# Second-block attention rewritten as sigmoids and a running product, with v2 and cuv ahead of conv

## What is computed

```python
y_a = a_b * short_conv(a_c * a_h, conv_w)
q = rms_norm(q per head, q_norm_g); k = rms_norm(k per head, k_norm_g)
z = q k^T * 64 ** -0.5
causal = s_pos < t_pos
log_beta = log_sigmoid(z)
log_rem = where(causal, log_sigmoid(-z), 0.0)
suffix = cumsum(log_rem, reverse=True) - log_rem
weights = where(causal, exp(log_beta + suffix), 0.0)
y_b = weights @ v
y_c = gelu(c_u) * (tril(sgu_w) @ rms_norm(gelu(c_v), g) + sgu_b)
h = h + concat(y_a, y_b, y_c) @ w_out
```

## Time and profile before

| what | value |
|---|---|
| median of three runs | 1559.61 us (1556.6 to 1559.64) |
| the profiled execution | 1554.32 us, span 1552.6 us |
| PE busy | 1220.0 us (79%) |
| DVE busy | 532.4 us (34%) |
| ACT busy | 393.1 us (25%) |
| POOL busy | 25.4 us (2%) |
| chain that ended last | DMA 44%, PE 39%, DVE 13%, ACT 2% |

### The profile page before, as it was taken

One profiled execution on the slowest core, in us unless ns is written; L12 is line 12 of the kernel. 1 busy time (PEld: TensorE's weight loads), 2 busy tenths in 40 slices (PEclk: granted clock), 3 DMA queues, 4 the chain that ended last, 5 costly groups with the idle time before them and its releaser, 6 DMA issues.

```text
span 1552.6 us, 20288 instructions
## 1 busy us (share of the span) xinstructions
PE 1220.0 (79%) x8432; PEld 786.5 (51%) x8432; DVE 532.4 (34%) x951; ACT 393.1 (25%) x622; POOL 25.4 (2%) x43
## 2 busy tenths in 40 slices
PE   8988798986676676676776676775766888999998
PEld 8866687743233233233232232232233776899886
DVE  6999677511001001001001001001001866666546
ACT  5646644300100100100100100100100465455434
POOL 1000021000000000000000000000000000000000
PEclk9999999988878778778778778778688998999999
DMA  8563223899999999999999999999999433555550
GB/s 293 190 217 98 87 102 149 352 413 429 430 429 431 431 429 431 432 429 430 432 431 430 430 431 431 431 428 431 432 431 423 155 109 135 187 174 183 190 190 28
DMA packets 58753, 493.39 MB, mean 318 GB/s; under 512 B 6930, under 2 KB 8268, under 8 KB 34124
## 3 DMA queue, kind: packets, MB, share of 16 engines
q1 hardware_dynamic: 57756, 491.61, 77.5%
q10 hardware_dynamic: 944, 1.05, 0.2%
HBM read 491.59 MB, written 1.05 MB: 317 GB/s over the span
## 4 chain that ended last, share of the span: by engine, by line
DMA 44%; PE 39%; DVE 13%; ACT 2%; issue 2%; DVEq 0%; SPq 0%; ACTq 0%
DMA ring<-in_expert_w_down 14%; DMA arena<-in_expert_w_down 11%; PE ps L1644 9%; DMA ring<-in_expert_w_up 7%; DMA ring<-in_expert_w_gate 7%; PE ps L1731 7%; PE ps L2010 7%; PE ps L1649 5%; PE ps L1994 3%; DVE w_split L986 3%; DMA arena<-in_expert_w_up 2%; DMA arena<-in_expert_w_gate 2%; PE ps L2028 2%; DVE stat L1111 1%; PE ps L1710 1%
## 5 line engine op out<-in xcount | busy, mean ns | idle before, releaser
L986 DVE TENSOR_TENSOR w_split<-ring,w_split 128x1024 fp32r<-128x1024 f32 (+3 forms) x178 | 200.8, 1141 | 92.3 <-ACT w_split L598 91.2
L598 ACT ACTIVATE w_split<-ring 128x1024 fp32r<-128x1024 f32 (+3 forms) x178 | 174.3, 988 | 199.0 <-PE ps L1649 145.8
L2010 PE MATMUL ps<-arena 128*32 128x512 f32 x1024 | 156.7, 760 | 66.5 <-DMA arena<-in_expert_w_up 64.7
L2010 PE MATMUL ps<-ring,arena 128*32 128x512 f32 x1024 | 153.5, 745 | 64.3 <-DMA ring<-in_expert_w_up 62.6
L1405 DVE TENSOR_TENSOR arena<-arena,ps 128x512 f32<-128x512 f32 x16 | 11.0, 687 | 441.7 <-PE ps L2010 441.7
L1412 DVE TENSOR_TENSOR xs<-ps,xs 128x512 f32<-128x512 f32 x64 | 39.7, 682 | 290.2 <-PE ps L2036 290.2
L1994 PE MATMUL ps<-arena,xn 128*128 128x32 f32 x512 | 104.1, 381 | 43.4 <-DVE arena L1389 43.4
L1994 PEld LDWEIGHTS ps<-arena,xn 128*128 128x128 f32 x512 | 102.0, 309 | 49.6 <-DVE arena L1389 26.5
L2010 PEld LDWEIGHTS ps<-arena 128*32 128x32 f32 x1024 | 33.6, 130 | 182.1 <-DMA arena<-in_expert_w_up 98.1
L2010 PEld LDWEIGHTS ps<-ring,arena 128*32 128x32 f32 x1024 | 33.3, 128 | 177.6 <-DMA ring<-in_expert_w_up 96.8
L1731 PE MATMUL ps<-hT_hi,w_split 128*128 128x256 f32 x608 | 110.3, 284 | 1.6 <-issue 0.8
(11 more groups left out here) (354 smaller groups left out, 1414.0 us busy)
## 6 DMA issues: line engine op xcount, KB each, us to landing
arena<-in_expert_w_gate SPq DMA_DIRECT2D x35, 2048.0 KB, 35.5
ring<-in_expert_w_up SPq DMA_DIRECT2D x35, 2048.0 KB, 36.0
arena<-in_expert_w_up SPq DMA_DIRECT2D x29, 2048.0 KB, 36.9
ring<-in_expert_w_gate SPq DMA_DIRECT2D x29, 2048.0 KB, 36.4
arena<-in_expert_w_down SPq DMA_DIRECT2D x25, 2048.0 KB, 29.4
ring<-in_expert_w_down SPq DMA_DIRECT2D x21, 2048.0 KB, 30.6
ring<-in_w_ff SPq DMA_DIRECT2D x32, 1024.0 KB, 5.1
ring<-in_w_in SPq DMA_DIRECT2D x24, 1024.0 KB, 5.0
```

Source lines behind the costliest of these rows:

```text
L598: act.activation(w_split[:, n % WBUFS, 0, 0:cols], slot_view(slot, cols)[:, n % 2, :], ACT.Copy).then_inc(split_hi, 1)
L986: dve.tensor_tensor(buf[:, 1, :], w, buf[:, 0, :].bitcast(F32), ALU.subtract).then_inc(split_lo, 1)
L2010: m = pe.matmul(ps[j * CAP:(j + 1) * CAP, bank, :], xe[:, kt, :], w[:, r, j * FCOL:(j + 1) * FCOL], start=kt == 0, stop=kt == KT - 1, skip ...
```

## The change

Attention is computed with the query on the partitions and the keys reversed on the free axis. ACT takes sigmoid(-z) (`left`) and sigmoid(z) (`taken`) from the scores directly. DVE multiplies `left` along the row with one `tensor_tensor_scan` (state = left * state + whole_stick, where `whole_stick` is 1 at the start of each block row and 0 elsewhere, and `left` is 0 there), and one product with `taken` gives the weights. The mask is added on PE: a matmul of `ident_r` and `never` adds -2^126 above the diagonal. The weights then have queries on the partitions, so PE turns them by six transposes a pair, ACT copies them to `wT`, and PE multiplies by v2.

cuv comes before conv and has its own banks (1 and 3, "C"); conv is interleaved with the pairs alone. qk2 is no longer copied before it is squared; the two norm gains are vectors over the partitions now, applied while ACT copies the turned q. Of out2 the rows that pairs 0 and 1 fill come first, conv next. The gating product in bank 1 waits for `conv_middle`, the first of DVE's reads of conv, instead of all. The suffix matmuls, the masks `tri` and `later`, and the four clock-keeping matmuls ahead of the last pair are gone.

```diff
-                        ("conv", "w_in_2", 0, 768, D, "A"), ("cuv", "w_in_2", 2304, 512, D, "A"),
+                        ("cuv", "w_in_2", 2304, 512, D, "C"), ("conv", "w_in_2", 0, 768, D, "A"),
+        ROW_ORDER = {"out2": (1, 0, 2, 3)}
+        MIXED_AT = {"pair": (0, 1, 4, 5), "conv": (2, 3)}
@@ ACT
-            evac("qk2", (qk2[:, 0, :], whole))
...
-            act.activation(sq, qk2.rearrange("p h d -> p (h d)"), ACT.Square).then_inc(sq_ready, 1)
+            for h in range(HALVES):
+                act.activation(sq[:, h * D:(h + 1) * D], pset(SETS["qk2"], h), ACT.Square,
+                               scale=rstd_x[:, h:h + 1]).then_inc(sq_ready, 1)
             high_parts("v2", 3)
-            high_parts("conv", 0, 3)
...
+            high_parts("cuv", 0, 6)
+            act.activation(lam_s[:, 0:1], rstd_0[:, 0:1], ACT.Gelu)
+            high_parts("cuv", 6)
+            high_parts("conv", 0, 2)
...
+                act.activation(qkT2[:, j, 0:T], ps[:, 4 + j, 0:T], ACT.Copy, scale=qk_w2)
+                act.activation(qkT2[:, j, T:2 * T], ps[:, 4 + j, T:2 * T][:, ::-1], ACT.Copy).then_inc(qkT2_evac, 1)
...
+            gelus(0)
+            act.wait_ge(qk_w2_ready, 1)
+            turned_qk(0)
+            turned_qk(1)
+            gelus(1)
+            act.activation(lam_s[:, 0:1], rstd_0[:, 0:1], ACT.Sigmoid)
+            turned_qk(2)
+            turned_qk(3)
+            high_parts("conv", 2, 4)
+            act.wait_ge(stick_cleared, 1)
+            sigmoids(0)
+            def sigmoids(p):
...
+                act.activation(rest[:, :, 1:P], z[:, :, 0:P - 1], ACT.Sigmoid, scale=-1.0)
+                act.activation(rest[:, :, P + 1:SC], z[:, :, P:SC - 1], ACT.Sigmoid, scale=-1.0).then_inc(left_ready, 1)
...
+                act.activation(taken[p % 2].rearrange("p (m c) -> p m c", m=2), z, ACT.Sigmoid).then_inc(taken_ready, 1)
@@ DVE
+            roots(ss_d, rstd_d, 4 * SHEADS, SHD, between=lambda: low_parts("v2", 5, 6))
+            low_parts("v2", 6, 7)
+            for h in range(HALVES):
+                n = slice(2 * SHEADS * h, 2 * SHEADS * (h + 1))
+                step(dve.tensor_scalar(rstd_d[:, n], rstd_d[:, n], rstd_x[:, h:h + 1], None, ALU.mult))
+            scaled_qk(0)
             low_parts("v2", 7)
+            dve.wait_ge(row_done, 1)
+            dve.tensor_copy(root_row, ps[:, 3, 0:T]).then_inc(row_read, 1)
+            low_parts("cuv", 0, 1)
+            scaled_qk(1)
+            low_parts("cuv", 1, 2)
+            evac_v2(0)
+            low_parts("cuv", 2, 3)
+            evac_v2(1)
+            low_parts("cuv", 3)
             low_parts("conv", 0, 3)
...
+            def conv_middle():
+
+                dve.wait_ge(tile_used, done("conv"))
+                dve.tensor_tensor(a_hT, a_c, r2, ALU.mult).then_inc(conv_read, 1)
...
+            def stick_weights(p):
...
+                dve.tensor_tensor_scan(stick, left[p % 2], whole_stick, 0.0, ALU.mult, ALU.add).then_inc(left_read, 1)
...
+                dve.tensor_tensor(blocks[0][:, :, ::-1], blocks[1], blocks[2], ALU.mult).then_inc(w_ready, 1)
...
+            low_parts("conv", 3, 4)
+            dve.wait_ge(stick_cleared, 1)
+            stick_weights(0)
+            low_parts("conv", 4, 6)
+            gating_sums()
+            stick_weights(1)
+            low_parts("conv", 6, 7)
+            split_pair(0)
+            gating_scale()
+            stick_weights(2)
+            low_parts("conv", 7)
+            split_pair(1)
+            low_parts("out2", 0, 1)
+            stick_weights(3)
+            low_parts("out2", 1, 2)
+            conv_middle()
+            split_pair(2)
+            conv_inputs()
+            low_parts("out2", 2, 3)
+            convolution(0)
+            convolution(1)
+            split_pair(3)
@@ PE
+            pe.wait_ge(diag_ready, HALVES)
+            pe.matmul(ps[:, 3, 0:T], ones[:, :], diag, start=True, stop=True).then_inc(row_done, 1)
             tiles("v2", hT)
...
+            pe.wait_ge(row_read, 1)
+            tiles("cuv", hT)
+            pe.wait_ge(qk2_ready, HALVES)
...
+                        pe.matmul(ps[:, 4 + m, at_col:at_col + width], qkT2[r, p, t0:t0 + P], qkT2[r, p, 2 * T - width:2 * T], start=True, stop=False)
+                        last = pe.matmul(ps[:, 4 + m, at_col:at_col + P], ident_r[:, :], never[:, :], start=False, stop=True)
...
+            tiles_T("conv", [0])
+            pe.wait_ge(qkT2_evac, 2)
+            pair_scores(0)
+            tiles_T("conv", [1, 2])
+            pair_scores(1)
+            pe.wait_ge(qkT2_evac, 4)
+            pair_turned(0)
+            tiles_T("conv", [3])
+            pe.wait_ge(gelu_done, 4)
+            pair_output(0)
+            pair_scores(2)
...
+            pair_turned(3)
             pe.wait_ge(pw_ready, 1)
             pe.wait_ge(cv_ready, 1)
-            pe.wait_ge(gelu_done, 4)
+            pe.wait_ge(conv_read, 1)
```

More of the change, by code:

```diff
@@ L423, in load_vec @@
                 src = t[name]
-                if name.startswith("diff"):
+                if name in HALF_ROWS:
+                    src = src if name.startswith("diff") else src[0:1]
                     for i in range(2):
@@ L528, in corner @@
             return pset(SETS[name], h)[:, j * 512:(j + 1) * 512]
+        raw_mask = hid[:, 0:P]
         @block.gpsimd
@@ L876, in _ @@
-            act.wait_ge(tile_used, done("cuv"))
-            for h in range(HALVES):
-                src = pset(SETS["cuv"], h)
-                act.activation(cv2[:, h, :], src[:, SGU:2 * SGU], ACT.Gelu, scale=rstd_x[:, h:h + 1]).then_inc(gelu_done, 1)
-                act.activation(u2[:, h, :], src[:, 0:SGU], ACT.Gelu, scale=rstd_x[:, h:h + 1]).then_inc(gelu_done, 1)
+            high_parts("cuv", 0, 6)
+            act.activation(lam_s[:, 0:1], rstd_0[:, 0:1], ACT.Gelu)
+            high_parts("cuv", 6)
@@ L886, in _ @@
+            sigmoids(1)
+            turned_weights(0)
+            high_parts("conv", 6, 7)
+            sigmoids(2)
+            high_parts("conv", 7)
+            turned_weights(1)
+            high_parts("out2", 0, 1)
+            sigmoids(3)
+            high_parts("out2", 1, 2)
+            turned_weights(2)
+            high_parts("out2", 2, 3)
+            turned_weights(3)
             high_parts("out2", 3, 7)
@@ L946, in step, with roots @@
                 dve.wait_ge(dve_step, count[0])
-            def roots(ss, out, n, dim, ready=None):
+            def roots(ss, out, n, dim, ready=None, between=None):
                 v, a, y = nw[0][:, 0:n], nw[1][:, 0:n], nw[2][:, 0:n]
@@ L960, in roots @@
                         step(last)
+                    if k == 0 and between is not None:
+                        between()
                 last.then_inc(ready, 1) if ready is not None else None
@@ L1610, in mixed @@
             def mixed(kt):
-                return (y_conv, kt + 1) if kt < 2 else (y_pair, kt - 1) if kt < 6 else (y_gate, 1)
+                for part, counted in (("pair", y_pair), ("conv", y_conv)):
+                    if kt in MIXED_AT[part]:
+                        return counted, MIXED_AT[part].index(kt) + 1
+                return y_gate, 1
             def transpose_bank(src, base, b, halves):
@@ L2134, in _ @@
             m.then_inc(sv_done, 1)
-            tiles("out2", yT, [4], ready=lambda kt: pe.wait_ge(*mixed(kt)))
+            y_part = lambda kt: pe.wait_ge(*mixed(kt))
+            pe.wait_ge(taken_ready, SHEADS // 2)
+            pair_output(3)
+            tiles("out2", yT, [0], ready=y_part)
+            tiles("out2", yT, range(1, 5), ready=y_part)
             pe.wait_ge(yc_ready, SG)
@@ L2140, in _ @@
             m.then_inc(ycT_done, 1)
-            tiles("out2", yT, range(5, KT), ready=lambda kt: pe.wait_ge(*mixed(kt)))
+            tiles("out2", yT, range(5, KT), ready=y_part)
             tiles("proj", pT)
```

288 lines of the change are left out of this document (128 added, 160 removed).

## The result

The changed kernel takes 1547.5 us (median of seven runs, 1541.84 to 1552.02) against 1556.6 us (1553.17 to 1559.64) for the kernel before in the same session: ratio 0.9938, 95% interval 0.9921 to 0.9955, so 9.1 us less where 21.2 were forecast. The time itself lies 0.5 us above the upper end of the range that the prediction gave, 1547. Of the distance to the forecast of 1538.4, 3.0 us go the other way: the forecast started from a median of three runs of the kernel before, 1559.61, and seven runs have 1556.6. The profiled execution took 1550.9 us with a span of 1548.7; the one before had 1552.6.

The account below looks back on a forecast made before the run. Back-and-forth between engines was taken as the limit. Terms A, B and C in a row ended at 1311.3 against 1336.6, 25.3 us less; with allowances 21.2 less, so 1538.4 us, range 1531 to 1547.

Parts of the forecast that it names:

- term B: DVE's own queue from the first scan until the gating product may start: 20.9 us, ending at 1278.5.
- at nothing: Small extra loads at the start, masks on GpSimd, its memsets and out2's new chunk order, all forecast to cost nothing.
- Term A: From qk2's end at 1225.0 until the first running product can start on DVE, forecast at 1257.6.
- its cover: PE's own queue alongside DVE's (conv tiles, scores, masks, turnings, outputs), forecast to reach 1278.0, level with DVE.
- rival 1: Each running product on DVE takes a second cycle an element, 3.2 us more on term B: 1541.6; chance 0.32.
- Term C: PE from the gating product to the end of the 16 "ff" transposes: 32.8 us.
- a slow stretch after stalls: Allowance for one stretch of slow PE clock after stalls of 1 to 2 us before the gating product: 3.4 us.
- Rival 2: PE stays at 1.2 GHz for two stretches more, 2 x 3.4 us: 1545.2; chance 0.12.
- Rival 3: No early release: gating product held by something else, PE waits for all conv_inputs (2.1 us): 1540.5; chance 0.05.

## Why the prediction was right and wrong

**Direction and mechanism: right.** The back-and-forth of the engines was the limit, and it is gone: PE idles 0.9 us after the end of qk2 where it had 15.2. The size was not right: the second block gave 16.4 of the 21.2, and the experts took 7.7 back. Two steps failed, the price of scores and masks in term B and the small vectors that were put at nothing.

**Term A: right.** The first scan was to start 32.6 us after qk2's end and started 32.1 after (1271.13 less 1239.0); cuv ended 23.8 after it, for 23.5. The table switch cost 1.28 us with the next call 0.02 behind, as the row of before had it. The drain that the Trainium skill (ScalarE: Activation LUTs, What ACT_TABLE_LOAD costs) adds does not show here.

**Term B: its cover failed.** I wrote "four scores with 16 mask matmuls of 0.06 to 0.17, so 3.4 + 1.6", and let DVE and PE be level at about 1278. The gating product started 62.2 us after qk2's end (1301.22 less 1239.0) where PE's queue gave 53.0: 9.2 late. The four pairs took 3.02 each and not 1.26, 7.0 in all. Clock is 1.7: 0.79 over 5 us and 0.67 over 2 is 1.2 GHz for 2.1 and 1.3 us. The two add to 8.7; the other 0.5 was not traced. The error was to take 0.86 for a pair's scores from rows in which four of them stand together, the two heads side by side, and a price per mask from rows in which matmuls of one kind follow one another, and to use both where two kinds alternate.

**The scan: rival 1's price was right, and it did not matter.** It takes 1.75 us, not the 0.96 I had taken. By this the trace agrees with the half throughput that the Trainium skill (DVE: opcode table, instruction layouts, handler registers and perf-mode slots, Datapath and trigger behaviour) states. But PE was the later of the two, so even a plain product moved nothing. Rival 1 reached 1541.6 by a path that was not the one that decides. DVE did have idle time between its scans, against what I wrote.

**Term C: right.** 32.8 forecast, 32.9 measured.

**The clock.** I allowed 3.4 us for a slow stretch after stalls. A loss of 1.7 came, while PE was without a gap. Rival 2's two stretches more did not come. Its reason was misread, too: PE did not stay at 1.2 GHz "after each stall over 1.5 us". The window from 1225 to 1245 holds a wait of 1.64 and has a clock of 1.00, and so has the one from 1287 to 1302, with a wait of 1.60 in it:

```profile
1294.30 0.73 PE L1649 MATMUL ps<-w_split,hT_hi 128*128 128x512 f32 x2 [1.60 <-DVE w_split L986]
```

**Rival 3, the early release: excluded.** In one profile it was worth 5 us and not the 2.1 of three products, since a loss of 3.3 by the clock came on top of the wait of 1.7; that the wait caused it is not shown. It is the only part of the change that was undone by itself, and it carries 5 of the second block's 16.4.

**At nothing: failed at one point.** The small vectors at the front were costed by their loads. I did not look at what lies behind them in memory, the arena, whose address moved by 480 bytes. The experts' 7.7 us take almost half of the gain of the second block: 16.4 less 7.7 is 8.7, and the medians differ by 9.1. The order of out2's chunks, also at nothing, was not taken back by itself, nor was cuv ahead of conv.

## What to carry to other kernels

When stalls between engines are removed, the length of the fullest queue is the new floor, so price the queue of TensorE in the order in which its instructions will stand, gather matmuls of equal row count, and put those that read different halves of the rows side by side. A price taken from rows of the kernel before holds for the order in which they stood there. And when a small buffer changes its size, look at where the large buffers land: here 480 bytes took back some 7 us of 16.

## What was not expected of the hardware

- Two f32 matmuls of 64 rows that read different halves of the partitions run at the same time when they stand side by side: two of 128 columns take 0.42 us where one takes 0.41, four (two of 128, two of 256) 0.86 where one by one they take 2.08.
- Matmuls of 64 and of 128 rows in turn are dear: a pair takes 1.36, 2.46 and 3.02 us with one, five and seven changes. After the lost overlap this leaves an estimated 0.17 us for each change at 2.4 GHz.
- Loads of the experts' weights run at 429 to 432 GB/s with the arena at 126720 and at 426 to 429 with it 32, 64 or 128 bytes beyond a multiple of 256; 898 against 903 to 907 us for the stretch.
- A scan of 768 elements takes 1754 ns, a product of the same size 955. A product whose output is written in reverse within blocks of 128 takes 958, as if it were not.
- The granted clock fell in the changed kernel (0.79 from 1267 to 1272, 0.67 from 1272 to 1274) although PE had been busy without a gap since 1255; other profiles of the same order of matmuls show no fall.
